# Output projection of a two-layer encoder trunk: seven block products instead of eight weight groups, and who subtracts their low parts

## What is computed

```
for l in range(DEPTH):                      # DEPTH = 2
    h = rms_norm(x, norm_mix[l])
    proj = h @ w_in[l]                      # q, k, v, u, gv
    att = window_attention(q, k, v, sinks[l])          # 512 x 512
    sgu = spatial_gating(gelu(u), gelu(gv), w_s[l], b_s[l])  # 512 x 512
    x = x + concatenate([att, sgu], axis=-1) @ w_o[l]  # 1024 x 1024
    h = rms_norm(x, norm_ffn[l])
    x = x + square(relu(h @ w_up[l])) @ w_down[l]      # 1024 x 4096 x 1024
return rms_norm(x, norm_final)
```

## Time and profile before

| | us |
|---|---|
| median of 3 runs | 966.22 |
| lowest and highest | 966.10 and 966.28 |
| the profiled execution | 966.15 |
| its span, first to last instruction | 964.1 |
| TensorE busy in the span | 952.1 (99%) |
| VectorE busy | 629.3 (65%) |
| ScalarE busy | 487.0 (51%) |
| GpSimd busy | 195.9 (20%) |
| mean granted clock of TensorE | 0.997 of full |

### The profile page before, as it was taken

How to read it: one execution, slowest core, us unless ns; L and a number is a source line. 1 busy time by engine, 2 the same in 40 slices (tenths; PEclk the granted TensorE clock), 3 DMA queues, 4 the chain that set the end, 5 groups by cost and what they waited for, 6 DMA issues and landing times.

```text
span 964.1 us, 11765 instructions
## 1 busy us (share of the span) xinstructions
PE 952.1 (99%) x4624; PEld 789.8 (82%) x4624; DVE 629.3 (65%) x822; ACT 487.0 (51%) x735; POOL 195.9 (20%) x122
## 2 busy tenths in 40 slices
PE   8999999999999999999999999999999999999996
PEld 5888789888888888888888888898888888888885
DVE  5675523679459558756948752446966784695586
ACT  5566424653554464355455663355445535544553
POOL 2554215110110010011147434231001001100100
PEclk9999999999999999999999999999999999999998
DMA  9332114975883875687244322079377568838832
GB/s 294 139 110 88 52 58 144 244 158 158 250 185 92 263 185 118 212 219 153 88 137 139 102 67 79 32 234 243 91 265 184 119 186 234 182 99 247 193 82 88
DMA packets 42648, 149.74 MB, mean 155 GB/s; under 512 B 5857, under 2 KB 5985, under 8 KB 42593
## 3 DMA queue, kind: packets, MB, share of 16 engines
q1 hardware_dynamic: 33088, 114.84, 35.3%
q0 software_dynamic: 9216, 33.56, 19.9%
q10 hardware_dynamic: 288, 0.59, 0.2%
HBM read 146.87 MB, written 2.10 MB: 155 GB/s over the span
## 4 chain that ended last, share of the span: by engine, by line
PE 93%; DVE 3%; ACT 1%; DMA 1%; issue 1%; POOL 0%; SPq 0%; DVEq 0%
PE bank L485 16%; PE bank L487 16%; PE bank L486 16%; PE bank L482 14%; PE bank L484 14%; PE bank L483 14%; DVE xt L1328 1%; PE bank L507 1%; DVE wlo L1073 1%; PE bank L626 1%; DMA xt<-x_in 1%; PE bank L661 1%; PE bank L671 1%; PE bank L652 1%; ACT z L809 0%
## 5 line engine op out<-in xcount | busy, mean ns | idle before, releaser
L485 PE MATMUL bank<-xhi,wlo 128*128 128x512 f32 (+1 forms) x720 | 271.7, 377 | 0.0
L487 PE MATMUL bank<-xlo,whi 128*128 128x512 f32 (+1 forms) x720 | 270.1, 375 | 0.0
L486 PE MATMUL bank<-xhi,whi 128*128 128x512 f32 (+1 forms) x720 | 270.0, 375 | 0.0
L796 ACT ACTIVATE whi<-raw 128x1024 fp32r<-128x1024 f32 x172 | 181.3, 1056 | 131.8 <-PE bank L484 113.0
L456 POOL TENSOR_TENSOR wlo<-raw,whi 128x1024 fp32r<-128x1024 f32 x52 | 140.1, 2706 | 213.1 <-ACT whi L796 213.1
L482 PE MATMUL bank<-wlo,fhi 128*128 128x512 f32 x448 | 174.5, 389 | 0.0
L484 PE MATMUL bank<-whi,flo 128*128 128x512 f32 x448 | 174.3, 389 | 0.0
L483 PE MATMUL bank<-whi,fhi 128*128 128x512 f32 x448 | 174.3, 389 | 0.0
L1073 DVE TENSOR_TENSOR wlo<-raw,whi 128x1024 fp32r<-128x1024 f32 x120 | 145.6, 1226 | 25.8 <-ACT whi L796 25.8
L463 POOL DMA_DIRECT2D raw<-weights_in x64 | 55.4, 866 | 512.1 <-DMA raw<-weights_in 503.0
L487 PEld LDWEIGHTS bank<-xlo,whi 128*128 128x128 f32 x720 | 135.6, 188 | 24.6
(11 more groups left out here) (108 smaller groups left out, 957.4 us busy)
## 6 DMA issues: line engine op xcount, KB each, us to landing
raw<-weights_in SPq DMA_DIRECT2D x172, 512.0 KB, 4.1
raw<-weights_in POOLq DMA_DIRECT2D x64, 512.0 KB, 6.8
rawx<-weights_in SPq DMA_DIRECT2D x32, 512.0 KB, 6.8
xt<-x_in SPq DMA_DIRECT2D x4, 512.0 KB, 8.3
gbc<-gains_in SPq DMA_DIRECT2D x4, 512.0 KB, 5.1
out_t<-xt SPq DMA_DIRECT2D x3, 512.0 KB, 2.6
gbc<-gains_in ACTq DMA_DIRECT2D x1, 512.0 KB, 5.7
wst<-ws_in SPq DMA_DIRECT2D x2, 256.0 KB, 6.9
```

The source lines that it names most:

```text
L485: pe.matmul(o, wlo[:, s, wc], hi[:, tokens], start=first, stop=False)
L486: pe.matmul(o, whi[:, s, wc], hi[:, tokens], start=False, stop=False)
L487: return pe.matmul(o, whi[:, s, wc], lo[:, tokens], start=False, stop=last)
L796: act.activation(whi[:, n % SLOTS, :], raw_at(slot), ACT.Copy).then_inc(whi_ready, 1)
```

## The change

The output projection becomes seven block products too, in both layers, with the functions of the MLP: quarter number `q = -1` stands for it. The blocks: A11 and A21 are the gating's 512 channels for the first and second half of the tokens, A12 and A22 the attention's (kept in a new buffer `mixed_at`). Seven products x 4 chunks x 2 token tiles x 3 = 168 matmuls in a layer instead of 192.

```diff
-GV_POS, K_POS, Q_POS, V_POS, U_POS, WO_POS, MLP_POS = 0, 4, 5, 9, 10, 14, 22
+GV_POS, K_POS, Q_POS, V_POS, U_POS, WO_POS, MLP_POS = 0, 4, 5, 9, 10, 14, 28
+WO_SLOT = (0, 2, 0, 0, 8, 2, 0)
+WO_LOW_BY_VECTOR = range(down_pos(-1, M2, 1), MLP_POS)
 def low_by_vector(n):
     if pos < MLP_POS:
-        return n < 2
+        return n < 2 or pos in WO_LOW_BY_VECTOR
...
-                mixed_half(l, mixed)
-                pe.wait_ge(att_lo, l * 4 + 4)
-                mixed_tiles(l, lambda t: turn(2 * l + 1, t - 1) if t else None)
+                for r in (M3, M4, M2, M1, M6):
+                    product(l, -1, r)
+                last_products(l, -1, lambda i: turn(2 * l + 1, i - 1) if i else None)
...
+                def difference(r):
+                    a11, a21, a12, a22 = (mixed_at[:, i, :, :] for i in range(4))
+                    one, other = {M2: (a21, a22), M1: (a11, a22), M6: (a21, a11), M5: (a12, a11), M7: (a12, a22)}[r]
+                    dve.wait_ge(att_copied, l * 4 + 4)
+                    dve.wait_ge(sgu_ready, l * 4 + 4)
+                    dve.tensor_tensor(differ[:, r % 2, :, :], one, other, ALU.subtract).then_inc(differ_ready, 1)
+                def difference_low(r):
+                    f = PRODUCTS[r][0] - A11
+                    dve.wait_ge(differ_hi, l * 5 + r - M4)
+                    dve.tensor_tensor(flo[:, f, :, :], differ[:, r % 2, :, :], fhi[:, f, :, :], ALU.subtract) \
+                        .then_inc(differ_lo, 1)
...
 def add_both(q, r):
-    add_product(q, r, 0)
-    add_product(q, r, 1)
+    if by_tiles(q, r):
+        add_product(q, r, 0)
+        add_product(q, r, 1)
+        return
+    dve.wait_ge(w_used, nth(l, down_pos(q, r, 1)) + 1)
+    for row, col, sign in PRODUCTS[r][2]:
+        block = xt[:, 2 * row:2 * row + 2, col * 512:(col + 1) * 512]
+        dve.tensor_tensor(block, block, pair[:, :, :], ALU.add if sign > 0 else ALU.subtract) \
+            .then_inc(x_added, 2)
...
+                difference(M2)
+                difference(M1)
+                low_down(-1, M2, 1)
+                difference_low(M2)
+                sum_m1(-1, 0)
+                sum_m1(-1, 1)
+                difference_low(M1)
+                low_down(-1, M1, 0)
+                difference(M6)
+                low_down(-1, M1, 1)
+                add_both(-1, M3)
+                difference_low(M6)
+                difference(M5)
+                low_down(-1, M6, 0)
+                add_both(-1, M4)
+                difference_low(M5)
+                low_down(-1, M6, 1)
+                difference(M7)
+                add_both(-1, M2)
+                low_down(-1, M5, 0)
+                low_down(-1, M5, 1)
+                difference_low(M7)
+                add_both(-1, M1)
+                low_down(-1, M7, 0)
+                low_down(-1, M7, 1)
+                add_both(-1, M6)
+                close_stage(-1, 2 * l + 1)
```

More of the change, by code:

```diff
@@ L103, in block_loads @@
 def block_loads(l, q, r, g):
-    slot = PRODUCT_SLOT[r] + g
+    slot = product_slot(q, r) + g
+    if q < 0:
+        return loads(l, slot) + WO_LOADS[r]
     late = 4 if r in (M6, M7) else 3 if r in (M3, M4) else 1
@@ L229, in build @@
         z = sb("z", [P, 2, SEQ])
[L230 to L232 removed]
+        rawx = sb("rawx", [P, 4, D])
+        sb("rest_2", [P, 768])
         raw = sb("raw", [P, 4, D])
@@ L422, in _ @@
             for l in range(DEPTH):
-                for pos in range(4 if l == 0 else 0, MLP_POS):
+                for pos in range(4 if l == 0 else 0, WO_POS):
                     load_mix(l, pos)
@@ L428, in _ @@
                         load_gain(2 * l + 1)
+                for r in (M3, M4, M2, M5, M6, M7):
+                    for g in range(2):
+                        load_block(l, -1, r, g)
                 for q in range(QUARTERS):
@@ L466, in _ @@
             for l in range(DEPTH):
-                for pos in range(2 if l == 0 else 0, MLP_POS):
+                for pos in range(2 if l == 0 else 0, WO_POS - 1):
                     low(nth(l, pos))
+                for g in range(2):
+                    add_block(l, -1, M3, g)
+                low(nth(l, WO_POS - 1))
+                for g in range(2):
+                    add_block(l, -1, M4, g)
+                for r in (M3, M4):
+                    for g in range(2):
+                        low(nth(l, down_pos(-1, r, g)))
+                low(nth(l, down_pos(-1, M2, 0)))
+                for r in (M6, M7):
+                    for g in range(2):
+                        add_block(l, -1, r, g)
                 for q in range(QUARTERS):
@@ L666, in attend @@
                 pe.wait_ge(pt_taken, l * 8 + 8)
-                for b in range(4):
+                for b in ATTEND_ORDER:
                     for n in range(2 * b, 2 * b + 2):
@@ L1329, in add_product, with wait_block @@
                                           ALU.add if sign > 0 else ALU.subtract).then_inc(x_added, 1)
-                def add_both(q, r):
-                    add_product(q, r, 0)
-                    add_product(q, r, 1)
+                def wait_block(q, r, k, row, col):
+                    before = [(p, i) for p in range(r) for i, at in enumerate(PRODUCTS[p][2]) if at[:2] == (row, col)]
+                    if before:
+                        p, i = before[-1]
+                        dve.wait_ge(x_added, added_block(l, q, p, k, i))
@@ new lines, in close_stage @@
+                def close_stage(q, norm):
+                    normed(norm, 0)
+                    normed(norm, 1)
+                    add_product(q, M5, 0)
+                    turned_low(norm, 0)
+                    add_product(q, M7, 0)
+                    normed(norm, 2)
+                    add_product(q, M5, 1)
+                    turned_low(norm, 1)
+                    add_product(q, M7, 1)
+                    turned_low(norm, 2)
+                    normed(norm, 3)
+                    turned_low(norm, 3)
```

355 lines of the change are left out of this document (166 added, 189 removed).

## The result

The changed kernel takes **978.95 us** (median of four runs, 978.85 to 979.27) against 966.17 of the kernel before in the same comparison: a ratio of 1.0133, 95% interval 1.0115 to 1.015. The forecast was 980.4, with a range of 974.5 to 986.0. Of all executions in this document one, the third of x8's four, took 1114.25 us at a mean granted clock of 0.80; the median given for x8 includes it (961.91 without it).

The account below looks back on a forecast made before the run. TensorE, busy for 99% of the span, was taken to bound the kernel. Per layer 5.44 us gained against 12.6 waited on VectorE's list and the close, 7.1 lost; 966.15 + 14.2 = 980.4 us, range 974.5 to 986.

Parts of the forecast that it names:

- 24 matmuls a layer, 10.9 us: TensorE, output projection: 24 of 192 matmuls removed per layer, worth 5.44 us each layer, 10.88 in both.
- 22 subtractions and 8 pair additions at 1.135: VectorE's list from the gating's end to M6's additions: 25.0 us of subtractions plus 9.1 of pair additions.
- Start of the list, 111.4: VectorE's list in layer 0 starts at 111.4, after ScalarE's cast of the last gating chunk and a 256-element subtraction.
- The hole, 1.05: VectorE idles 1.05 us in its list, waiting for ScalarE's cast for the low part of M2's second tile.
- The exclusion, 2.4: GpSimd's low part of M2's first tile locks VectorE out of SBUF, costing its list 2.40 us.
- M6's first addition, 148.9: VectorE, layer 0: sum of list start, subtractions, pair additions, idle time and lockout puts this addition at 148.9.
- The close, 13.8 from that addition to the MLP's first matmul: Projection's end, layer 0: addition ends at 149.6, first normalised tile ready at 152.7, MLP's first matmul at 162.7.
- 7.1 a layer: MLP's first matmul comes 7.1 us later per layer: 5.44 gained, 12.6 waited; 14.2 for both layers.
- The loads: Extra weight DMAs are hidden; only the MLP's first tile might come late, up to 1.8 us a layer, taken as 0.
- Full gain: Rival: TensorE is never starved in the projection, giving 955.3 us; chance 0.09 for full gain or most of it.
- No exclusion: Rival: same chain without VectorE and GpSimd locking each other out, 2 x 2.4 less, 975.6 us; chance 0.08.
- The clock: Rival: new waits in the projection make TensorE's clock fall, some 5 us a layer, 990 us; chance 0.05.

Follow-up runs that it names:

- x8: x7 with four low parts given to GpSimd, each held by a semaphore until VectorE's pair additions, and some reordering; 962.13 us, ratio 0.9956.
- x6: Changed kernel with 21 of VectorE's 22 listed subtractions cut to 32 columns, numbers not the reference's; 956.34 us, ratio 0.990.
- x5: Changed kernel with the low parts of the five differences cut to 32 of 1024 columns, numbers not the reference's; 968.69 us, ratio 1.0026.
- x10: Changed kernel with the projection's additions of M3, M4, M2 and M1 done by single banks instead of pairs; 979.74 us.
- x1: Changed kernel with GpSimd's low part of M2's first tile cut to 32 of 1024 columns; 974.75 us, ratio 1.009.
- x4: Changed kernel with M6's additions ahead of M7's two low parts in VectorE's list; 979.57 us, ratio 1.0138.
- x7: x2 with the differences of M2 and M1 waiting only for the attention's second half, M2's moved to the front; 972.53 us, ratio 1.0065.
- x3: Changed kernel with the six low parts of M6, M5 and M7 given back to GpSimd; median 974.87 us, ratio 1.0103.
- x2: Changed kernel with the low part of M2's first tile moved from GpSimd to VectorE; 974.63 us, ratio 1.0089.
- x9: x8 with GpSimd's four subtractions released by their casts alone, not held back for VectorE's additions; 970.93 us, ratio 1.0037.
- x11: x8 repeated unchanged with more rounds; 961.92 us, ratio 0.9957.

## Why the prediction was right, step by step

- *What bounds the kernel.* TensorE stays the bound only as long as its operands come: right. x6 shows the other half, the full gain when they do.
- *24 matmuls a layer, 10.9 us.* 9.35 of them in x6's projections, where a wait of 0.4 a layer for the last transposed tile is left.
- *22 subtractions and 8 pair additions at 1.135.* The rows give 2.27 and 2.26 for two. The subtractions are shown by x5 (1.03 each for what was cut), the additions by x10.
- *Start of the list, 111.4.* It was 111.02, 0.4 earlier: TensorE reached the projection 0.13 sooner, and the last gating chunk's cast began at 110.23 instead of at 110.6.
- *The hole, 1.05.* 0.94, on the cast of M2's second tile, as said.
- *The exclusion, 2.4.* 2.20 in the profile, 2.1 a layer by x1. The bounds were 0 and 2.4, and the row from which I took the upper one (GpSimd gets in between two VectorE instructions that stand back to back) was the right one.
- *M6's first addition, 148.9.* 148.27; the 0.6 are the three terms above.
- *The close, 13.8 from that addition to the MLP's first matmul.* 162.06 - 148.27 = 13.79. x4 adds what I had not seen: M7's low parts and products end hardly earlier than the norm's chain, so a gain on the one is soon a wait for the other.
- *7.1 a layer.* 6.49 and 6.63, then 0.5 less behind the last matmul. For the pair additions in the MLP I had put nothing, since VectorE isn't waited for there; in the last quarter its list ends the kernel, and my 8 x 0.065 = 0.5 come back in full. Hence 978.9 and not 980.4.
- *The loads.* ScalarE did wait 0.86 us for the MLP's first tile, and as reckoned it fell in time that the next step had to spare: the close still took 13.79.
- *Rivals.* Full gain: no. No exclusion: refuted by x1. That TensorE would wait four or five times within 20 us, and where: right (132.54 to 152.12, and once more for `xlo`). Their rows add up to 10.2 us a layer where 5.4 + 6.5 = 11.9 were lost, since a row counts a wait from the modelled end of the matmul before it, not from when the next could have started.
- *The clock.* Here my reason was weaker than the result. I set it at 5% because no wait is as long as the silence at the end. In after's profile the clock is indeed 1.00 behind a wait of 2.70 us. But in x7's it falls to 0.50 behind one of 2.67, in x3's behind one of 2.42, and in the profiles of x1 and x2 it falls in layer 1 and not in layer 0, behind a wait of 2.7 in either. The other three executions of after have mean clocks of 0.993 to 0.997 against the 0.998 of the profiled one, at the same time to 0.4 us. So it very likely falls there too, behind M7's wait, and is hidden by VectorE's chain, as x10's profile shows it for nearly the same kernel; no profile of after itself shows it. The price that I gave, 5 us a layer, was too high: in x7 the fall lasts some 3 us and is covered, and in x3, where less is covered, the execution with the lowest clock is 5.2 us longer than the fastest one, for both layers together. That the time came out right with the clock at nothing owes something to this cover, which I had not reckoned for a fall as short as that.
- *Slips.* M1's first low part is the ninth instruction of the list and not the eleventh (the time of 125 was right), six subtractions are 6.8 us and not yet the 7.1 from which the change pays, and from M6's first low part to M5's it takes eight VectorE instructions, from M5's to M7's five, not six each (131.27, 140.34 and 146.00 in after). None of them was a term of the sum.

The Trainium skill, "TensorE: Matmul & The Clock Gate", Part 1, lets the clock fall after an idle spell. The falls of x3 and x7 came after waits shorter than the one that after's profile shows without a fall, so the length of the single wait doesn't tell it.

What remains open is whether after's clock falls in its other executions, what made most of x3's executions faster than its profile shows, and when the clock falls at all.

## What to carry to other kernels

Count the busy time of the engine that has to feed the faster one, from the moment at which its inputs exist, not over the stage: VectorE had 29 us free in this stage before the change, and they lay ahead of the work. Work that goes to an idle engine isn't free when both engines read SBUF: one subtraction left on GpSimd cost 2.1 us a layer where VectorE would have done it in 1.135; placed beside VectorE's additions from PSUM the same kind of instruction cost nothing. The timing alone was worth 8.8 us (x8 against x9), the clock's part in it. Together with x2's and x7's moves and four subtractions handed over, it turned 13 us lost into 4 won. When a list on one engine sets the end, the cheapest gains are its holes and what can run ahead of it (x2, x7), before any instruction is taken away.

## What the runs showed of the hardware

- VectorE and GpSimd exclude each other for whole instructions when VectorE's has both inputs in SBUF, and not when one is in PSUM. Caught VectorE instructions of 1.22 took 3.39 to 3.43 in layer 0 (x3, x9), and a tile's normalisation with its inputs `xt` and `gbc` in SBUF, 1.28 otherwise, took 3.12 in x3. Two additions from PSUM took 2.34 beside GpSimd, as alone (x8). So the two engines wait for one another without a semaphore too. The Trainium skill, "SBUF — State Buffer", section "SBUF: two separate sides", names the first case, an instruction of VectorE with two SBUF inputs against a GpSimd one that reads SBUF; the traces agree with it.
- In the projections of these runs no GpSimd subtraction waited longer than to the end of the second VectorE instruction (4.27 for 2.40 at the most, x9), though VectorE's stand back to back.
- TensorE's clock can fall to the lower of its two levels (granted clock 0.50, 1.2 GHz) and come back within the projection, for some 3 to 7 us. It did so in the profiles of x1, x2, x3, x4, x7, x9 and x10, behind waits of 2.1 to 4.1 us, and not in after's behind one of 2.70, nor in those of x8 and x11, whose longest wait there is 1.30. It differs between executions of one kernel: x3 and x9 spread over 5.2 and 3.7 us, and their slower executions have the lower mean clocks, while x1 and x7, where VectorE's chain covers the fall, keep within 0.3.
